# A residual transformer block on one core: the first slab of the up projection taken on tokens that carry no norm factor yet

## The chip, the cores and the metric

The kernel runs on 1 core of one Trainium2 chip. The metric is the device time of one execution in microseconds (us), the median of several runs. The engines are PE (TensorE, products), ACT (ScalarE), DVE (VectorE), POOL (GpSimd) and SP (the queue that issues the transfers).

## The reference

256 tokens of width 1024 pass a first block (two kinds of attention, a gated convolution feed-forward part, a gated embedding) and a second block (convolution, sparse attention, pooling, a mixture of 32 experts). The change lies at the start of the first block's feed-forward part:

```
x = x + rms_norm(mix, g_post_mix[i])

h = rms_norm(x, g_pre_ffn[i])
u = causal_depthwise_conv(h @ w_up[i], conv_w[i], conv_b[i])
gate, val = jnp.split(u, 2, axis=-1)
f = (jax.nn.gelu(gate, approximate=True) * val) @ w_down[i]
```

`rms_norm(x, g)` is `x * g` times one factor per token, 1/sqrt(mean(x*x) + eps). The factor depends on the token alone, so `(x * g) @ w_up` may be multiplied by it afterwards.

## The kernel before

Each engine has its own hand-written list of instructions, and they meet only through semaphores. Every engine runs its list in order, so an instruction that waits holds back all that is written behind it on its engine. There is no planner: the order in the code is the order on the chip.

**The tokens** lie with features on the partitions: `xT` has 8 tiles of 128 features x 256 tokens (in the trace the name is `xg`, which holds it). After the output projection `wo`, PE turns its result over, 16 products of 128x128 (`to_features`), and DVE adds it to `xT` tile by tile (`add_turned`, 8 instructions). Then the norm: ACT squares `xT` in 4 pieces, PE sums them with a matrix of ones (`token_sums`), ACT copies the sums, PE makes a column of them (`token_columns`), ACT takes the root, DVE its reciprocal, and PE spreads the factor over all partitions (`turned_over`, bank 3). DVE then makes `h` = x * gain * factor per tile (yT).

**Rounded pairs.** The large products run on operands rounded to fp32r, in two parts: a rounded one (hi, made by ACT) and the rest (lo, the original minus hi, made by DVE or POOL). One product of two numbers is three: hi*hi, hi*lo, lo*hi. So each tile of `h` has an `x_hi` (ACT) and an `x_lo` (DVE).

**The up projection** `w_up` comes in 11 slabs (j), each of 8 tiles (k) of 128 rows x 512 columns. Per tile ACT rounds the weights (`up_rounded`, 128x512), DVE or, for the tiles in `POOL_UP`, POOL makes the rest, and PE runs 12 products of 128x256. The rounded weights have 4 places (`weight_place`, two in `fr`, two in `fr_h`), so tile n is rounded only when PE has done with tile n-4. A slab's result fills two PSUM banks (`up_bank`): half 0 (gate) and half 1 (value). In slab j+1 its convolution follows (`conv_step` on three engines): ACT makes a base for each half (`conv_base`), DVE adds 2 taps to each half (`conv_tap`, 8 instructions per slab), ACT takes the gelu of half 0, POOL multiplies the halves (f), ACT rounds f (`f_hi`), POOL makes its rest (`f_lo`). The bank is free for slab j+2 after that.

**After slab 0** ACT also takes the silu of a vector (`crow`) that SP loads into `sq` when the norm's squares have been read. SP issues the loads of the slabs 3 to 6 behind that one. `mod_sum(1)` (a DVE copy) and `mod_total(1)` (PE, then DVE) finish a second vector product that only needs the slots of an earlier stage; before, they stand in the gap of the norm. `idle_products` are products whose result nobody reads.

Of the kernel before, what the change touches and what calls it, by code (L numbers as in the profile page):

```python
# [15 lines left out]
S = 256  # L16
# [45 lines left out]
POOL_UP = {("lo", 0, k) for k in (0, 1, 2, 3, 5, 7)} | {("lo", j, k) for j in range(1, 11) for k in (3, 7)}  # L62
# [100 lines left out]
def build(nc, A, out):  # L163
    with ExitStack() as ctx:
# [118 lines left out]
        OB = (6, 7)  # L283

# [24 lines left out]
        FB = (0, 1, 4, 5)  # L309
# [12 lines left out]
        def up_bank(j, part_):  # L322
            return FB[(2 * j + part_) % 4]

# [149 lines left out]
        def tensor(pe):  # L474
# [35 lines left out]
            def mod_total(s, *free):  # L510
                pe.wait_ge(dve_mod["sum", s], *free)
                for c in range(4):
                    t = pe.matmul(ps[:, 5, 4 * c:4 * c + 4], ar[:, modp + 128 * c:modp + 128 * c + 128], ident[:, 0:128:32], True, True)
                t.then_inc(pe_mod, "total", s)
# [255 lines left out]
            pe.wait_ge(act_wo["root", 1])  # L770
            idle_products(1, 5)
            token_sums("mix", 2, dve_joint["mix", "mt", 1, 0])
            idle_products(1, 5)
            token_columns("mix", 2)
            idle_products(2, 5)
            pe.wait_ge(dve_joint["mix", "rrecip"])
            turned_over(3, misc[:, 118:120]).then_inc(pe_joint, "mix", "over")
            mod_total(1, act_wo["root", 1])


            for j in range(11):
# [61 lines left out]
            embed(0, 0, dve_up["conv", 9, 1])  # L843
            pe.wait_ge(dve_up["conv", 10, 1])
# [4 lines left out]
            mod_half(10, 0, dve_up["conv", 9, 1])  # L849
# [377 lines left out]
        def scalar(act):  # L1227
# [212 lines left out]
            x_squares("mix")  # L1440
            joint_row("mix", 2, 116)
            for k in range(8):
                act.wait_ge(dve_up["h", k])
                act.copy(tile(fr, k, XH), tile(yT, k)).then_inc(act_up, "x_hi", k)


            def conv_base(j, p):
                act.wait_ge(pe_up[j, 7], pool_up["f_lo", j - 2] if j > 1 else dve_up["x_lo", 7])
                for i in range(2):
                    f = 2 * j + i + 22 * p  # L1450
                    act.activation(conv_place(j, p)[:, S * i:S * i + S], half(up_bank(j, p), i), ACT.Identity, scale=col("conv_w", 88 + f),
# [249 lines left out]
        def vector(dve):  # L1701
# [144 lines left out]
            def mod_total(s):  # L1846
                turned = ps[:, 5, 0:16].rearrange("p (c q) -> p q c", q=4)
# [103 lines left out]
            mod_total(1)  # L1951
# [15 lines left out]
            def conv_tap(j, p, d):  # L1967
                for i in range(2):
                    f = 2 * j + i + 22 * p
                    y, u = conv_place(j, p)[:, S * i:S * i + S], half(up_bank(j, p), i)  # L1970
# [14 lines left out]
            for j in range(11):  # L1985
                for k in range(8):
                    if ("lo", j, k) not in POOL_UP:
                        hi, lo = weight_place(8 * j + k)
                        dve.wait_ge(act_up["hi", j, k])
                        dve.tensor_tensor(lo, slot("wup", j)[:, 512 * k:512 * k + 512], hi.bitcast(F32), ALU.subtract).then_inc(dve_up, "lo", j, k)  # L1990
                    if j:
# [827 lines left out]
```

## Time and profile before

| what | value |
|---|---|
| median of 3 runs | 926.48 us (925.8 to 926.95) |
| span of the profiled execution, first to last instruction | 923.0 us |
| the runs' median over the span: 926.48 - 923.0 | 3.5 us |
| busy share PE / DVE / ACT / POOL | 85% / 41% / 35% / 14% |
| instructions | 12738 |

The profile is one execution. Its span is what the trace shows; the 3.5 us are what lies around the span in a run, and the page gives no time of its own for the profiled execution beside it. Busy shares are means over stages with different limits. A row of the timeline is a start, a duration, the engine, the code line, the operation with its result and inputs, and a count; in brackets stands the idle time of that engine before it and what ended it. A product in plain fp32 shows as two records.

### The profile page before, as it was taken

The numbers are of one execution on the slowest core, as the hardware profiler recorded it, in microseconds if no ns is written. First come the engines' busy times: TensorE is split into PE (matmuls) and PEld (weight loads), VectorE is DVE, ScalarE is ACT, GpSimd is POOL, SyncE is SP. The second block draws the span as 40 slices with busy tenths as digits, with TensorE's granted clock in tenths as the row PEclk, the third lists the DMA queues.
The fourth block names the chain that finished last, engine by engine and source line by source line (L and its number), as shares of the span: only waits on it lengthen the run. The fifth ranks groups of instructions, "written<-read, shape, count | busy, mean of one in ns | idle before, by whom it ended". The sixth has DMA issues, their size and how long they took to land.

```text
span 923.0 us, 12738 instructions
## 1 busy us (share of the span) xinstructions
PE 780.4 (85%) x5320; PEld 527.5 (57%) x5320; DVE 382.2 (41%) x837; ACT 327.2 (35%) x652; POOL 126.1 (14%) x129
## 2 busy tenths in 40 slices
PE   9999999999999999999999996567765576755756
PEld 7986588999998867798785432122220222211214
DVE  5747766667779764899613110010100101001002
ACT  5756756666665466824723010001000000000003
POOL 0011031555541034102110000000000000000000
PEclk9999999999999999999999999887797888979868
DMA  9956708754069782655679999999999999999996
GB/s 356 416 186 229 320 0 356 277 185 184 28 250 397 298 318 93 251 184 205 240 288 357 428 426 430 426 428 427 430 426 426 430 429 426 427 430 430 425 426 250
DMA packets 25263, 298.48 MB, mean 323 GB/s; under 512 B 2800, under 2 KB 3184, under 8 KB 6512
## 3 DMA queue, kind: packets, MB, share of 16 engines
q1 hardware_dynamic: 25200, 297.61, 78.5%
q8 instruction: 43, 0.70, 0.3%
q14 instruction: 20, 0.16, 0.1%
HBM read 296.55 MB, written 1.05 MB: 322 GB/s over the span
## 4 chain that ended last, share of the span: by engine, by line
PE 59%; DMA 33%; ACT 4%; DVE 3%; issue 1%; SPq 0%; DVEq 0%; ACTq 0%
PE ps L108 58%; DMA ring<-in_exps 33%; ACT fr L117 1%; PE ps L111 1%; ACT sq L114 1%; ACT ar L117 1%; ACT ar L114 0%; DVE ar L126 0%; DVE fr L126 0%; ACT L114 0%; DVE xg L134 0%; DVE yT L134 0%; DVE misc L149 0%; DVE yT L126 0%; DVE yT L130 0%
## 5 line engine op out<-in xcount | busy, mean ns | idle before, releaser
L108 PE MATMUL ps<-fr 128*128 128x256 f32 (+2 forms) x1308 | 206.6, 314 | 1.4 <-ACT fr L114 0.4
L108 PE MATMUL ps<-ring,sq 128*32 128x512 f32 x944 | 137.7, 719 | 78.3 <-DMA ring<-in_exps 77.9
L108 PEld LDWEIGHTS ps<-fr 128*128 128x128 f32 (+1 forms) x1308 | 182.9, 189 | 19.4 <-DVE fr L126 2.2
L108 PE MATMUL ps<-ring,ar 128*32 128x512 f32 (+4 forms) x792 | 93.5, 562 | 41.2 <-DMA ring<-in_exps 35.0
L108 PEld LDWEIGHTS ps<-ring,sq 128*32 128x32 f32 x944 | 28.7, 120 | 174.4 <-DMA ring<-in_exps 121.4
L126 DVE TENSOR_TENSOR fr<-ring,fr 128x512 fp32r<-128x512 f32 (+2 forms) x121 | 93.8, 804 | 42.9 <-ACT fr L117 42.6
L126 DVE TENSOR_TENSOR ar<-ar,ps 128x512 f32<-128x512 f32 x9 | 6.2, 687 | 254.4 <-PE ps L108 254.4
L117 ACT ACTIVATE fr<-ring 128x512 fp32r<-128x512 f32 (+1 forms) x139 | 80.1, 622 | 25.3 <-PE ps L108 23.1
L117 ACT ACTIVATE ar<-ps 128x512 f32<-128x512 f32 (+4 forms) x48 | 27.2, 571 | 171.2 <-PE ps L111 147.9
L108 PEld LDWEIGHTS ps<-ring,ar 128*32 128x32 f32 (+1 forms) x792 | 26.2, 117 | 93.5 <-DMA ring<-in_exps 53.1
L108 PE MATMUL ps<-ar 128*128 128x512 f32 (+10 forms) x328 | 66.4, 421 | 7.9 <-DVE ar L126 6.8
L126 DVE TENSOR_TENSOR ar<-ps,ar 128x512 f32<-128x512 f32 (+6 forms) x38 | 23.4, 633 | 108.8 <-PE ps L108 108.5
L114 ACT ACTIVATE sq<-ps,misc 128x128 f32<-128x128 f32 x31 | 11.9, 457 | 158.4 <-PE ps L108 158.4
L108 PE MATMUL ps<-fr,fr_h 128*128 128x256 f32 x528 | 66.9, 283 | 0.0
L108 PEld LDWEIGHTS ps<-fr,fr_h 128*128 128x128 f32 x528 | 64.9, 192 | 0.0
L108 PEld LDWEIGHTS ps<-ar 128*128 128x128 f32 (+4 forms) x328 | 37.1, 173 | 39.6 <-issue 19.2
L126 POOL TENSOR_TENSOR ar<-ar 128x128 f32<-128x128 f32 (+2 forms) x21 | 11.2, 535 | 310.8 <-DVE ar L126 309.7
L117 ACT ACTIVATE fr_h<-ring 128x512 fp32r<-128x512 f32 x66 | 40.2, 630 | 17.6 <-PE ps L108 17.6
L114 ACT ACTIVATE ar<-ps 128x768 f32<-128x768 f32 (+1 forms) x21 | 15.0, 717 | 81.1 <-PE ps L108 80.1
L108 PEld LDWEIGHTS ps<-ar,yT 128*128 128x128 f32 x256 | 32.6, 203 | 14.3 <-issue 14.1
L134 DVE SCALAR_TENSOR_TENSOR yT<-ps,cols,yT 128x255 f32<-128x255 f32 (+1 forms) x88 | 37.2, 474 | 0.0
L126 DVE TENSOR_TENSOR fr_h<-ring,fr_h 128x512 fp32r<-128x512 f32 x43 | 31.3, 730 | 13.5 <-ACT fr_h L117 13.5
(187 smaller groups left out, 908.9 us busy)
## 6 DMA issues: line engine op xcount, KB each, us to landing
ring<-in_exps SPq DMA_DIRECT2D x84, 2048.0 KB, 30.8
ring<-in_modw SPq DMA_DIRECT2D x12, 2048.0 KB, 13.1
ring<-in_wup SPq DMA_DIRECT2D x11, 2048.0 KB, 12.7
ring<-in_wdown SPq DMA_DIRECT2D x5, 2048.0 KB, 13.1
ring<-in_exps SPq DMA_DIRECT2D x9, 1024.0 KB, 10.4
ring<-in_win SPq DMA_DIRECT2D x4, 2048.0 KB, 11.3
ar<-in_exps SPq DMA_DIRECT2D x3, 2048.0 KB, 12.6
ring<-in_wo SPq DMA_DIRECT2D x2, 2048.0 KB, 8.7
```

The source lines that it names most:

```text
L108: return Issue(self.e and self.e.matmul(o, l, r, start=start, stop=stop, skip_group_check=True))
L111: return Issue(self.e and self.e.transpose(o, i, ident))
L114: return Issue(self.e and self.e.activation(o, i, f, **kw))
L117: return Issue(self.e and self.e.activation(o, i, ACT.Copy, scale=scale))
L126: return Issue(self.e and self.e.tensor_tensor(o, a, b, op))
L134: return Issue(self.e and self.e.scalar_tensor_tensor(out=o, in0=a, scalar=s, in1=b, op0=op0, op1=op1))
```

## The change

Slab 0 takes its products on x * gain without the token's factor ("raw": `raw_hi` on ACT, `raw_rest` on DVE), so PE can begin it as soon as x is there. In slab 0 the norm's factor is made: ACT squares x between the raw tiles, POOL adds the 4 pieces of squares to one (3 instructions), PE makes the columns from it between tiles 5 and 6 (`mix_columns`) and spreads the factor between tiles 6 and 7. DVE copies the factor row to SBUF (`rb`), multiplies the two halves of slab 0's result by it (`raw_out`, 2 instructions, into SBUF in place of PSUM), and makes `h` for the slabs 1 to 10, whose `x_hi` and `x_lo` are made within slab 1. So in slab 1, too, PE runs lo products of the tokens last in each tile. The convolution of slab 0 moves: its bases into slab 1, its taps, gelu, product and f into slab 2, beside those of slab 1, and they read SBUF (`ar`) and not PSUM. The silu moves behind slab 3. POOL now has the tiles 0 to 3 of slab 0 and 0 to 3 and 7 of slab 1. `mod_sum(1)` and `mod_total(1)` move up into the `wo` stage, the idle products go, and SP's wait before `crow` and the slabs 3 to 6 is now for the columns.

```diff
-POOL_UP = {("lo", 0, k) for k in (0, 1, 2, 3, 5, 7)} | {("lo", j, k) for j in range(1, 11) for k in (3, 7)}
+POOL_UP = {("lo", 0, k) for k in range(4)} | {("lo", 1, k) for k in range(3)} | {("lo", j, k) for j in range(1, 11) for k in (3, 7)}
...
-        FB = (0, 1, 4, 5)
+        RH, RL = 11264, 13312
+        FB = (4, 5, 0, 1)
...
+        def up_out(j, part_):
+            return bank(up_bank(j, part_)) if j else ar[:, RH + 512 * part_:RH + 512 * part_ + 512]
...
                         column_sums(5, [(tile(sq, k), act_wo["osq", k // 2]) for k in range(4)]).then_inc(pe_wo, "sums", 1)
+                        mod_total(1)
                         pe.wait_ge(act_wo["sums", 1])
...
-            pe.wait_ge(act_wo["root", 1])
-            idle_products(1, 5)
-            token_sums("mix", 2, dve_joint["mix", "mt", 1, 0])
-            idle_products(1, 5)
-            token_columns("mix", 2)
-            idle_products(2, 5)
-            pe.wait_ge(dve_joint["mix", "rrecip"])
-            turned_over(3, misc[:, 118:120]).then_inc(pe_joint, "mix", "over")
-            mod_total(1, act_wo["root", 1])
...
+            def mix_columns():
+                pe.wait_ge(pool_joint["mix", "squares", 3])
+                for j in range(2):
+                    for m in range(2):
+                        o = 256 * m + 128 * j
+                        t = pe.matmul(ps[:, 2, S + j:S + j + 1], sq[:, o:o + 128], ones[:, 0:1], j == 0 and m == 0, m == 1)
+                t.then_inc(pe_joint, "mix", "cols")
...
-                    if j == 0:
-                        pe.wait_ge(act_up["x_hi", k])
+                    xh, xl = (tile(fr, k, o) for o in ((XH, XL) if j else (RH, RL)))
+                    if j < 2:
+                        pe.wait_ge(act_up["x_hi" if j else "raw_hi", k])
                     for m in range(4):
...
-                            pe.wait_ge(dve_up["conv", j - 2, m // 2] if j > 1 else
-                                       (dve_mod["mod", 1] if m // 2 else dve_mod["sum", 1]) if j else dve_joint["mix", "x", 7])
+                            pe.wait_ge(*((dve_up["conv", j - 2, m // 2],) if j > 2 else (dve_up["raw", m // 2],) if j == 2 else
+                                         (dve_joint["mix", "x", 7],) if j else (dve_mod["mod", 1], act_wo["root", 1])))
...
-                        xh, xl = tile(fr, k, XH), tile(fr, k, XL)
...
-                        if j:
+                        if j > 1:
...
-                        t = pe.matmul(o, wl[:, c], xh, False, j > 0 and k == 7)
-                    if j == 0:
-                        pe.wait_ge(dve_up["x_lo", k])
+                        t = pe.matmul(o, wl[:, c], xh, False, j > 1 and k == 7)
+                    if j < 2:
+                        pe.wait_ge(dve_up["x_lo" if j else "raw_lo", k])
...
-                            t = pe.matmul(o, wh[:, c], tile(fr, k, XL), False, k == 7)
+                            t = pe.matmul(o, wh[:, c], xl, False, k == 7)
...
                     t.then_inc(pe_up, j, k)
+                    if (j, k) == (0, 5):
+                        mix_columns()
+                    if (j, k) == (0, 6):
+                        pe.wait_ge(dve_joint["mix", "rrecip"])
+                        turned_over(3, misc[:, 118:120]).then_inc(pe_joint, "mix", "over")
...
-            x_squares("mix")
-            joint_row("mix", 2, 116)
-            for k in range(8):
...
+            def raw_input(k):
+                act.wait_ge(dve_joint["mix", "x", k])
+                act.copy(tile(fr, k, RH), tile(xT, k), col("g_pre_ffn", k)).then_inc(act_up, "raw_hi", k)
...
+            for i in range(4):
+                raw_input(2 * i)
+                raw_input(2 * i + 1)
+                act.activation(sq[:, i * 512:(i + 1) * 512], xT[:, i * 512:(i + 1) * 512], ACT.Square).then_inc(act_joint, "mix", "xsq", i)
+                if i:
+                    up_rounded(0, 3 + i)
+            up_rounded(0, 7)
+            up_rounded(1, 0)
+            act.wait_ge(pe_joint["mix", "cols"])
+            row_root(misc[:, 116:118], ps[:, 2, S:S + 2], 1024).then_inc(act_joint, "mix", "rroot")
+            up_rounded(1, 1)
...
-                act.wait_ge(pe_up[j, 7], pool_up["f_lo", j - 2] if j > 1 else dve_up["x_lo", 7])
+                act.wait_ge(pool_up["f_lo", j - 2] if j > 1 else None, pe_up[j, 7] if j else dve_up["raw", p],
+                            dve_up["x_lo", 7 if j else 2 * p + 1])
...
-            for j in range(11):
+            normed_input(0)
+            up_rounded(1, 2)
+            normed_input(1)
+            normed_input(2)
+            up_rounded(1, 3)
+            conv_base(0, 0)
+            normed_input(3)
+            up_rounded(1, 4)
+            normed_input(4)
+            conv_base(0, 1)
+            up_rounded(1, 5)
+            normed_input(5)
+            normed_input(6)
+            up_rounded(1, 6)
+            normed_input(7)
+            up_rounded(1, 7)
+            for j in range(2, 11):
                 for k in range(8):
-                    if j or k > 3:
-                        up_rounded(j, k)
-                    if j:
-                        conv_step(j - 1, k)
-                if j == 0:
+                    up_rounded(j, k)
+                    if j == 2 and k in (2, 5):
+                        conv_step(0, 5 if k == 2 else 7)
+                    conv_step(j - 1, k)
+                if j == 3:
                     act.wait_ge(landed["crow"]["all"])
...
             mod_total(0)
+            mod_sum(1)
...
             group_factor(1)
+            mod_total(1)
...
-            for k in range(8):
-                add_turned("mix", k, (6, 7, 0, 1)[k // 2], col("g_post_mix", k))
-            joint_row("mix", 116)
-            mod_sum(1)
...
+            def raw_rest(k):
+                dve.wait_ge(act_up["raw_hi", k])
+                dve.scalar_tensor_tensor(tile(fr, k, RL), tile(xT, k), col("g_pre_ffn", k), tile(fr, k, RH).bitcast(F32),
+                                         ALU.mult, ALU.subtract).then_inc(dve_up, "raw_lo", k)
+
+            def raw_out(p):
+
+                dve.wait_ge(pe_up[0, 7], dve_joint["mix", "row"])
+                dve.tensor_tensor(by(up_out(0, p), S), by(bank(up_bank(0, p)), S), wide(rb[:, 1, :], 2), ALU.mult).then_inc(dve_up, "raw", p)
+
+            def normed(k):
+                dve.wait_ge(dve_joint["mix", "row"])
+                dve.scalar_tensor_tensor(tile(yT, k), tile(xT, k), col("g_pre_ffn", k), rb[:, 1, :], ALU.mult, ALU.mult).then_inc(dve_up, "h", k)
+
+            def normed_rest(k):
+                dve.wait_ge(act_up["x_hi", k])
+                dve.tensor_tensor(tile(fr, k, XL), tile(yT, k), tile(fr, k, XH).bitcast(F32), ALU.subtract).then_inc(dve_up, "x_lo", k)
...
+            def up_rest(j, k):
+                if ("lo", j, k) not in POOL_UP:
+                    hi, lo = weight_place(8 * j + k)
...
             for k in range(9):
                 if k < 8:
-                    dve.wait_ge(pe_joint["mix", "over"])
-                    dve.scalar_tensor_tensor(tile(yT, k), tile(xT, k), col("g_pre_ffn", k), half(3, 0), ALU.mult, ALU.mult).then_inc(dve_up, "h", k)
+                    add_turned("mix", k, (6, 7, 0, 1)[k // 2], col("g_post_mix", k))
                 if k:
-                    dve.wait_ge(act_up["x_hi", k - 1])
-                    dve.tensor_tensor(tile(fr, k - 1, XL), tile(yT, k - 1), tile(fr, k - 1, XH).bitcast(F32), ALU.subtract).then_inc(
-                        dve_up, "x_lo", k - 1)
-            mod_total(1)
+                    raw_rest(k - 1)
+                if k == 6:
+                    up_rest(0, 4)
+            for k in range(5, 8):
+                up_rest(0, k)
+            joint_row("mix", 116)
...
-            for j in range(11):
+            dve.wait_ge(pe_joint["mix", "over"])
+            dve.tensor_copy(rb[:, 1, :], half(3, 0)).then_inc(dve_joint, "mix", "row")
+            normed(0)
+            for k in range(1, 9):
+                if k < 8:
+                    normed(k)
+                normed_rest(k - 1)
+                if k in (2, 3):
+                    raw_out(k - 2)
+                if k in (4, 5, 6):
+                    up_rest(1, k)
+            for j in range(2, 11):
...
+                    up_rest(j, k)
+                    if j == 2 and k < 3:
+                        for d in ((1, 2), (1,), (2,))[k]:
+                            conv_tap(0, int(k > 0), d)
+                    conv_step(j - 1, k)
...
-            for j in range(11):
+            for k in range(4):
+                t = rest(pool_up, ("lo", 0, k), slot("wup", 0)[:, 512 * k:512 * k + 512], *weight_place(k), t, act_up["hi", 0, k])
+            for i in range(1, 4):
+                pool.wait_ge(t, act_joint["mix", "xsq", i])
+                t = pool.tensor_tensor(sq[:, 0:512], sq[:, 0:512], sq[:, 512 * i:512 * i + 512], ALU.add).then_inc(pool_joint, "mix", "squares", i)
+            for j in range(1, 11):
...
-                    if j:
+                    if j > 1:
+                        if j == 2 and k in (4, 6):
+                            t = conv_step(0, 6 if k == 4 else 7, t)
                         t = conv_step(j - 1, k, t)
...
-                    sp.wait_ge(pe_joint["mix", "sums"])
+                    sp.wait_ge(pe_joint["mix", "cols"])
```

On DVE, behind the turning over at the end of `wo`; `xg<-ps,cols,xg` is an add of `add_turned`, `fr<-xg,cols,fr` a `raw_rest`, `fr<-ring,fr` and `fr_h<-ring,fr_h` the rest of a weight tile of slab 0:

```order
-L134 SCALAR_TENSOR_TENSOR xg<-ps,cols,xg 128x256 x8
+L134 SCALAR_TENSOR_TENSOR xg<-ps,cols,xg 128x256 x2
...
+L134 SCALAR_TENSOR_TENSOR fr<-xg,cols,fr 128x256
+L126 TENSOR_TENSOR fr<-ring,fr 128x512
+L134 SCALAR_TENSOR_TENSOR xg<-ps,cols,xg 128x256
+L134 SCALAR_TENSOR_TENSOR fr<-xg,cols,fr 128x256 x2
+L126 TENSOR_TENSOR fr<-ring,fr 128x512
+L126 TENSOR_TENSOR fr_h<-ring,fr_h 128x512 x2
 L137 RECIPROCAL misc<-misc 128x2
```

The adds were one run of 8; now each is followed by a raw rest, and the rests of the weight tiles 4 to 7 stand among and behind them.

On POOL, from the rests of slab 0's first tiles on; `sq<-sq` are the adds of the squares, `yT<-yT` a product f of the convolution, `fr<-yT,fr` its rest:

```order
 L126 TENSOR_TENSOR fr_h<-ring,fr_h 128x512 x2
-L126 TENSOR_TENSOR fr<-ring,fr 128x512
-L126 TENSOR_TENSOR fr_h<-ring,fr_h 128x512 x2
+L126 TENSOR_TENSOR sq<-sq 128x512 x3
+L126 TENSOR_TENSOR fr<-ring,fr 128x512 x2
+L126 TENSOR_TENSOR fr_h<-ring,fr_h 128x512 x4
 L126 TENSOR_TENSOR yT<-yT 128x512
-L126 TENSOR_TENSOR fr_h<-ring,fr_h 128x512
 L126 TENSOR_TENSOR fr<-yT,fr 128x512
-L126 TENSOR_TENSOR fr_h<-ring,fr_h 128x512
 L126 TENSOR_TENSOR yT<-yT 128x512
 L126 TENSOR_TENSOR fr_h<-ring,fr_h 128x512
```

Two products f and the first f's rest now stand before tile 7 of slab 2 (the last `fr_h` row), with no weight tile between them.

On ACT, first a piece of slab 2, then what stands at the end of slab 3; `fr<-ring` and `fr_h<-ring` are weight tiles (the two `fr_h` rows around the first table load are the tiles 2 and 3 of slab 2), `yT<-yT` is a gelu, `fr<-yT` an `f_hi`, `sq<-sq` the silu:

```order
+L117 ACTIVATE fr_h<-ring 128x512
+L114 ACT_TABLE_LOAD
+L114 ACTIVATE yT<-yT 128x512
+L117 ACTIVATE fr_h<-ring 128x512
...
+L117 ACTIVATE fr<-yT 128x512
 L114 ACT_TABLE_LOAD
 L114 ACTIVATE sq<-sq 128x1024
...
 L117 ACTIVATE fr<-ring 128x512 x2
 L114 ACT_TABLE_LOAD
```

Before, the silu with its load stood behind slab 0, ahead of the first gelu and its load; now the load for slab 0's gelu comes first, between two weight tiles, then the silu's behind slab 3 and ahead of slab 4's weights, then a gelu's again: one load more.

## Rows read from the trace of the kernel before

**Rows 1.** The page's chain that ended last, by engine.

```profile
PE 59%; DMA 33%; ACT 4%; DVE 3%; issue 1%; SPq 0%; DVEq 0%; ACTq 0%
```

**Rows 2.** Busy time in stretches: start:end, length, PE, PEld, DVE, ACT, POOL, clock, DMA share, GB/s.

```profile
137.30:144.34 7.04, 6.19 (x44) 3.63 (x42) 3.97 (x11) 3.64 (x8) 0.77 (x1) 1.00 0.38 126
144.34:156.28 11.94, 11.83 (x97) 11.63 (x97) 8.60 (x19) 8.23 (x15) 2.92 (x2) 1.00 1.01 432
156.28:167.80 11.52, 11.52 (x99) 11.52 (x97) 7.37 (x14) 8.66 (x15) 5.70 (x4) 1.00 1.01 430
167.80:179.30 11.50, 11.50 (x98) 11.50 (x97) 8.02 (x15) 7.36 (x14) 5.80 (x5) 1.00 0.53 190
```

**Rows 3.** The chain in order of time: start, duration, what.

```profile
150.43 200.57 PE ps L108 x1374
...
553.36 30.16 DMA ring<-in_exps
```

**Rows 4.** Timeline of PE around the norm.

```profile
113.61 0.70 PE L108 MATMUL ps<-sd,con 128*128 128x256 f32 x2 [0.94 <-ACT sd L117]
...
137.37 0.39 PE L108 MATMUL ps<-con 128*128 128x128 f32 x2
...
142.51 0.71 PE L108 MATMUL ps<-con,misc 128*128 128x128 f32 x4
143.10 1.06 PE L108 MATMUL ps<-con,ar 128*128 128x4 f32 x8
144.34 3.11 PE L108 MATMUL ps<-fr 128*128 128x256 f32 x24 [0.18 <-ACT fr L117]
```

**Rows 5.** Timeline of DVE and POOL, a later stage with the raw rest's form.

```profile
335.87 4.10 POOL L126 TENSOR_TENSOR fr<-ring,fr 128x512 fp32r<-128x512 f32 x3
...
337.35 0.47 DVE L134 SCALAR_TENSOR_TENSOR xg<-ps,cols,xg 128x256 f32<-128x256 f32 x1
337.74 1.09 DVE L134 SCALAR_TENSOR_TENSOR fr<-xg,cols,fr 128x256 fp32r<-128x256 f32 x1
...
340.57 0.47 DVE L134 SCALAR_TENSOR_TENSOR fr<-xg,cols,fr 128x256 fp32r<-128x256 f32 x1
```

**Rows 6.** Timeline of ACT, a later stage with the raw tile's form.

```profile
336.07 0.91 ACT L117 ACTIVATE fr<-xg,cols 128x256 fp32r<-128x256 f32 x2
```

**Rows 7.** Timeline of DVE, slabs 0 and 1, and the adds before them.

```profile
136.30 3.23 DVE L134 SCALAR_TENSOR_TENSOR xg<-ps,cols,xg 128x256 f32<-128x256 f32 x8 [0.87 <-PE ps L108]
...
144.22 0.43 DVE L126 TENSOR_TENSOR fr<-yT,fr 128x256 fp32r<-128x256 f32 x1
...
150.72 1.43 DVE L126 TENSOR_TENSOR fr_h<-ring,fr_h 128x512 fp32r<-128x512 f32 x1 [0.35 <-ACT fr_h L117]
154.14 1.29 DVE L126 TENSOR_TENSOR fr<-ring,fr 128x512 fp32r<-128x512 f32 x2 [1.99 <-ACT fr L117]
158.67 1.64 DVE L134 SCALAR_TENSOR_TENSOR yT<-ps,cols,yT 128x255 f32<-128x255 f32 x4
```

**Rows 8.** Timeline of POOL, slabs 0 and 1.

```profile
150.31 1.29 POOL L126 TENSOR_TENSOR fr<-ring,fr 128x512 fp32r<-128x512 f32 x1 [12.25 <-ACT fr L117]
...
163.25 1.60 POOL L126 TENSOR_TENSOR yT<-yT 128x512 f32<-128x512 f32 x1 [3.26 <-DVE yT L134]
164.92 1.29 POOL L126 TENSOR_TENSOR fr_h<-ring,fr_h 128x512 fp32r<-128x512 f32 x1
```

**Rows 9.** Timeline of ACT, slabs 0 and 1.

```profile
151.23 1.28 ACT L114 ACT_TABLE_LOAD   x1
152.53 1.06 ACT L114 ACTIVATE sq<-sq 128x1024 f32<-128x1024 f32 x1
...
165.41 1.14 ACT L117 ACTIVATE fr<-ring 128x512 fp32r<-128x512 f32 x2
168.00 1.02 ACT L114 ACTIVATE yT<-ps,cols 128x256 f32<-128x256 f32 x2 [1.45 <-PE ps L108]
```

**Rows 10.** Timeline of SP.

```profile
141.28 1.90 SPq L160 DMA_DIRECT2D ring<-in_wup  x4
```

More of the change, by code:

```diff
@@ L283, in build @@
         OB = (6, 7)
+        TOTAL_BANK = (5, 4, 5)
         part_place = [fr[:, vm:vm + 1024], fr_r[:, 2048:3072], fr_r[:, 3072:4096], fr[:, wT:wT + 1024], fr[:, vS:vS + 1024],
@@ L512, in mod_total @@
                 for c in range(4):
-                    t = pe.matmul(ps[:, 5, 4 * c:4 * c + 4], ar[:, modp + 128 * c:modp + 128 * c + 128], ident[:, 0:128:32], True, True)
+                    t = pe.matmul(ps[:, TOTAL_BANK[s], 4 * c:4 * c + 4], ar[:, modp + 128 * c:modp + 128 * c + 128], ident[:, 0:128:32], True, True)
                 t.then_inc(pe_mod, "total", s)
@@ L841, in gate @@
                 pe.matmul(o, xh, wl, False, k == 7).then_inc(pe_gate, j, n, k)
-            embed(0, 0, dve_up["conv", 9, 1])
-            pe.wait_ge(dve_up["conv", 10, 1])
+            embed(0, 0, dve_up["conv", 10, 1])
             to_features("ffn", (0, 1, 2, 3))
@@ L848, in tensor @@
             embed(1, 1, act_gate["e", 1, 0])
-            mod_half(10, 0, dve_up["conv", 9, 1])
+            mod_half(10, 0)
             pe.wait_ge(act_gate["e", 1, 1], dve_joint["ffn", "mt", 1, 1])
@@ L1439, in scalar, with normed_input @@
             up_rounded(0, 3)
-            x_squares("mix")
-            joint_row("mix", 2, 116)
-            for k in range(8):
+            def raw_input(k):
+                act.wait_ge(dve_joint["mix", "x", k])
+                act.copy(tile(fr, k, RH), tile(xT, k), col("g_pre_ffn", k)).then_inc(act_up, "raw_hi", k)
+            def normed_input(k):
                 act.wait_ge(dve_up["h", k])
                 act.copy(tile(fr, k, XH), tile(yT, k)).then_inc(act_up, "x_hi", k)
+            for i in range(4):
[9 more added lines that the diff above has]
+            up_rounded(1, 1)
             def conv_base(j, p):
-                act.wait_ge(pe_up[j, 7], pool_up["f_lo", j - 2] if j > 1 else dve_up["x_lo", 7])
+                act.wait_ge(pool_up["f_lo", j - 2] if j > 1 else None, pe_up[j, 7] if j else dve_up["raw", p],
+                            dve_up["x_lo", 7 if j else 2 * p + 1])
                 for i in range(2):
                     f = 2 * j + i + 22 * p
-                    act.activation(conv_place(j, p)[:, S * i:S * i + S], half(up_bank(j, p), i), ACT.Identity, scale=col("conv_w", 88 + f),
+                    act.activation(conv_place(j, p)[:, S * i:S * i + S], up_out(j, p)[:, S * i:S * i + S], ACT.Identity, scale=col("conv_w", 88 + f),
                                    bias=col("conv_b", f)).then_inc(act_up, "base", j, p, i)
@@ L1846, in mod_total @@
             def mod_total(s):
-                turned = ps[:, 5, 0:16].rearrange("p (c q) -> p q c", q=4)
+                turned = ps[:, TOTAL_BANK[s], 0:16].rearrange("p (c q) -> p q c", q=4)
                 o = (mod[:, 32:48] if s else mod[:, 16:32]).rearrange("p (q c) -> p q c", c=4)
@@ L1943, in vector @@
+            def up_rest(j, k):
+                if ("lo", j, k) not in POOL_UP:
+                    hi, lo = weight_place(8 * j + k)
+                    dve.wait_ge(act_up["hi", j, k])
+                    dve.tensor_tensor(lo, slot("wup", j)[:, 512 * k:512 * k + 512], hi.bitcast(F32), ALU.subtract).then_inc(dve_up, "lo", j, k)
             for k in range(9):
                 if k < 8:
-                    dve.wait_ge(pe_joint["mix", "over"])
-                    dve.scalar_tensor_tensor(tile(yT, k), tile(xT, k), col("g_pre_ffn", k), half(3, 0), ALU.mult, ALU.mult).then_inc(dve_up, "h", k)
+                    add_turned("mix", k, (6, 7, 0, 1)[k // 2], col("g_post_mix", k))
@@ L1969, in conv_tap @@
                     f = 2 * j + i + 22 * p
-                    y, u = conv_place(j, p)[:, S * i:S * i + S], half(up_bank(j, p), i)
+                    y, u = conv_place(j, p)[:, S * i:S * i + S], up_out(j, p)[:, S * i:S * i + S]
                     dve.wait_ge(act_up["base", j, p, 1] if d == 1 else dve_up["tap", j, p, i])
@@ L1983, in conv_step @@
                     conv_tap(j, 1, 2)
-            for j in range(11):
-                for k in range(8):
[L1987 to L1990, printed above, removed]
-                    if j:
-                        conv_step(j - 1, k)
+            dve.wait_ge(pe_joint["mix", "over"])
[10 more added lines that the diff above has]
+            for j in range(2, 11):
+                for k in range(8):
+                    up_rest(j, k)
[3 more added lines that the diff above has]
+                    conv_step(j - 1, k)
                     if j > 6 and k == 1:
@@ L2343, in gpsimd @@
                                  act_up["hi", j, k])
-                    if j:
+                    if j > 1:
+                        if j == 2 and k in (4, 6):
+                            t = conv_step(0, 6 if k == 4 else 7, t)
                         t = conv_step(j - 1, k, t)
```

## Prediction

> **What bounds the kernel now.** I read the chain that ended last first. By engine it is PE for 59% and DMA for 33% [rows 1]; in order of time it is PE without a break from 150.43 us for 200.57 us, and from 553.36 us on it is the loads of the expert weights [rows 3]. So the stretch that the change touches is bound by PE. The loads at the end are issued as PE gives places of the ring free, so a shift of PE at 150 us should move their start, and the end, by as much; I take one to one.
>
> The stretches say how full PE is [rows 2]. In 137.30 to 144.34, the norm, PE shows 6.19 us busy, but with idle products, sums and columns. Slab 0 runs from 144.34 to 156.28, slab 1 to 167.80, slab 2 to 179.30. In slabs 1 and 2 PE is busy the whole time, 96 products in 11.5 us or 0.12 us each, at the full clock (granted 1.00). The other engines have 11.5 us per slab, too, and DVE's 8.02 and POOL's 5.80 hide only as long as each result comes in time. How much time that is, is the question here.
>
> **What is removed.** PE ends the turning over at 137.37 and begins slab 0 at 144.34 [rows 4]. The first raw tile is ready about then: the adds begin at 136.30 and take 0.40 each (3.23 for 8) [rows 7], a raw tile on ACT takes some 0.42 (0.91 for 2 in a row) [rows 6]. So slab 0 can begin at 137.4: **-7.0 us**.
>
> **What is added on PE.** The columns: 4 products, 8 records, near the row of 8 small ones, 1.06 [rows 4]: 1.0. The spreading, 0.71 for 4 records [rows 4]: 0.6 until the next product. `mod_total(1)`, 1.06 [rows 4], moves into a wait of 0.94 ahead of 113.61 [rows 4], with a DVE copy ahead of the group norm. Between 0.1 (1.06 - 0.94) and 0.8 (a copy of 0.7 all on the path, plus that); I take 0.2, since PE has 84 products of old tiles to run meanwhile.
>
> **What it does to the others.** No row shows the new order, so I lay it out: every engine's list in its written order, each instruction starting when its engine is free and its last input is there. Durations from rows, back to back: DVE 0.40 for 128x256 with a scalar, 0.61 for 128x512 (1.29 for 2, where 0.69 and 0.60 follow each other, an overlap of some 0.08), and by that overlap 0.35 for the plain subtraction of 0.43 [rows 7]; ACT 0.52 for a weight tile (1.14 for 2), 0.45 for a base (1.02 for 2) [rows 9]; POOL 1.30 [rows 8]. Laid out so, the old order gives slab ends of 156.3, 167.8, 179.4 and 190.9; the rows have 156.28, 167.80, 179.30, so the layout carries such waits.
>
> One more thing goes into it. DVE and POOL hold each other up. A DVE instruction with two tensors in SBUF, the raw rest's form, takes 0.47 alone and 1.09 while POOL works; one with a PSUM input takes 0.47 beside the same POOL work [rows 5]. The weight rest at 150.72 takes 1.43 and ends after POOL's at 150.31 to 151.60 [rows 7, 8]. The change makes many such instructions: 8 raw rests, `h` from the copied row in SBUF and not from PSUM, 8 taps of slab 0 from SBUF, and 3 adds on POOL that did not exist. Of `h` and the taps no row shows that they are held. The Trainium skill ("SBUF — State Buffer", "Who interferes with whom") has any DVE instruction with two SBUF inputs contend with a GpSimd one that reads SBUF, and none with one SBUF input. By the row's two forms alone the layout ends 0.4 us earlier than by that rule; I take all of them as held.
>
> - *Slab 0.* Before tile 4's weight rest DVE has 7 adds and 6 raw rests (5.2 us from 136.30), waits 0.3 and 0.55 for ACT's raw tiles, which stand behind squares and weight tiles, and is held by two of POOL's adds (0.4 and 1.1). The rest is done at 144.36, PE wants it at 143.1: 1.26. Tile 5's is behind another add and two raw rests, 0.60 late. Slab 0 ends at 137.37 + 11.52 + 1.26 + 0.60 + 1.6 + 0.1 = 152.5, **3.8 us ahead** of 156.3.
> - *Slab 1.* The factor leaves PE at 151.0, the row copy and the first `h` and `x_hi` take 1.4, 0.1 of it on PE. Then DVE has 8 `h`, 8 `x_lo`, 2 raw outputs, 3 weight rests, 3.2 + 2.8 + 1.2 + 1.8 = 9.0 us of 11.5, with 2 us of being held and a turn to ACT and back for each tile. PE waits 0.44 for the third `x_lo`, 0.28, 0.72 and 1.46 for the weight rests of tiles 5, 6 and 7: tile 7 is rounded behind the last `x_hi`, at 164.0, and POOL adds 1.3. Sum 3.0; the slab ends at 167.0, **0.8 ahead**.
> - *Slab 2.* ACT loads the gelu's table, 1.28 [rows 9], and runs slab 0's gelu between the weight tiles 2 and 3: tile 3 is 1.19 late. DVE has 16 taps (8 take 3.3 by 1.64 for 4 [rows 7]), so slab 1's product f comes late on POOL, and tile 7 behind it: 1.14; tile 6 0.26. In the old order POOL's tile 7 ends at 166.21 [rows 8] for a PE that wants it at 166.4, so there was 0.2 to give. Sum 2.6, the end at 181.15, **1.8 behind**.
> - *Slab 4.* In the old order the first weight tiles of a slab are rounded at 165.41, 2.4 before the slab begins at 167.80 [rows 2, 9], and need 0.63 and a DVE rest of 0.69. Table load and silu, 1.28 + 1.0 [rows 9], now stand ahead of them: 2.3 + 1.3 - 2.4 = **1.2 late**. Before, they stood at 151.23, where ACT then waited for PE. For a table switch the Trainium skill ("ScalarE: Activation LUTs", "Table sets: the hidden batching unit") gives some 2.7 us, an estimate of 2.4 us more on the sum; the trace has 1.28, and the sum goes by that.
>
> SP's loads of slabs 3 to 6, at 141.28 [rows 10], go out behind the columns, some 8 us later; slab 3's weights are wanted at about 178, so 30 us hide it; without that cover it is the 8.
>
> Sum: slab 4 ends 1.8 + 1.2 = 3.0 us later than before, and nothing changes behind it. With the 0.2 of `wo`, **+3.2 us**. On the profiled span, 923.0 + 3.2 = 926.2; the runs lie 3.5 above it, so **929.7 us**, 0.35% slower. With the durations moved by 2 to 6% the layout's +3.0 stays within 2.4 and 3.9.
>
> **Rivals.**
> 1. *DVE and POOL don't hold each other in the new places.* Without any of it the layout ends 1.2 ahead, with `wo` 1.0: 925.5 us. For it: no row shows `h` or the taps beside POOL. Against it: the raw rest's own form is held [rows 5], and weight rests are [rows 7]. If POOL's adds of the squares alone escape, +1.7, 928.2.
> 2. *PE stays fed, faster.* The waits of the slabs 1, 2 and 4 (3.0 + 2.6 + 1.2 = 6.8) are each a chain of small handovers between ACT, DVE and POOL. If the weight rests come early enough, only slab 0's costs remain: -3.8 + 0.2 = -3.6, 922.9 us. It decides once those waits fall under 1.7 together, for then it is over 0.2% faster. For it: DVE and ACT are not full over a slab [rows 2]. Against it: the order is fixed, and the slack of POOL's tile 7 was 0.2 us.
> 3. *The delay does not reach the end.* From 553.36 the loads bound [rows 3]; had they been issued ahead of need, a late PE would cost nothing: 926.5. Against it: they are issued when PE frees their places.
>
> **How the numbers follow.** A difference of 0.2% (1.9 us) is about what a measurement of this kernel tells from none. The forecast, with its own range of 928.6 to 930.7, has 0.68, rival 1 0.14, rival 2 0.14, rival 3 0.04. A hundredth of rival 1 lies beyond the bound, at partial holding. So slower 0.69, same 0.17, faster 0.14. The range leaves rival 2 out and reaches down to rival 1, 925.4, and up to 931.3, the layout's worst and 0.8 in `wo`.
>
> **What the profile will show.** Right: PE's first `fr` products at 137.4 to 137.6; slab 0 (its end by the first wait for `raw_out`) at 152 to 153; PE waiting 3 us in slab 1 and over 2 in slab 2, for POOL in the last tile of each; 1 us ahead of slab 4, for ACT and DVE behind the silu; raw rests of over 1 us beside POOL's adds. From slab 5 on 11.5 us per slab. Wrong: slab 1 ending before 165, raw rests and `h` at 0.47 beside POOL, or no wait ahead of slab 4; then the layout's handovers are too slow. A longer `wo` stage would show as a turning over that ends later than 137.6.

## The result and the profile after

The changed kernel takes 930.22 us (median of 5 runs, 928.75 to 931.38) against 926.48 (925.8 to 927.2, 5 runs): the ratio is 1.004 with a 95% interval of 1.0028 to 1.0052, or 3.7 us more. Slower was the likeliest forecast, at 929.7. One of the nine executions of the kernel without POOL's adds, below, took 1486.27 us; its ratio leaves that one out, and the median of the other eight is 928.20 for 928.30.

The page's chain that ended last, by engine, answers to [rows 1]; PE has lost four points of it, most of them to ACT and DVE (5% each, for 4% and 3%).

```profile
PE 55%; DMA 33%; ACT 5%; DVE 5%; POOL 1%; issue 1%; POOLq 0%; DVEq 0%; ACTq 0%
```

The chain in order of time shows what took them: where before it was PE alone from 150.43 us [rows 3], it now goes from engine to engine, mostly one short instruction each, and PE has it alone only from 195.14 on. Its DMA tail begins at 557.84 instead of 553.36 [rows 3].

```profile
164.33 0.63 ACT fr_h L117
165.09 1.28 POOL fr_h L126
166.41 1.71 PE ps L108 x12
...
195.14 160.27 PE ps L108 x1038
...
557.84 30.40 DMA ring<-in_exps
```

The timeline of PE, answering to [rows 4]: a bracket is the idle time ahead of the row and what ended it.

```profile
107.24 1.05 PE L108 MATMUL ps<-con,ar 128*128 128x4 f32 x8
...
138.26 3.15 PE L108 MATMUL ps<-fr 128*128 128x256 f32 x24
...
145.63 1.69 PE L108 MATMUL ps<-fr 128*128 128x256 f32 x12 [1.35 <-DVE fr L126]
147.69 1.70 PE L108 MATMUL ps<-fr 128*128 128x256 f32 x12 [0.38 <-DVE fr L126]
149.23 0.95 PE L108 MATMUL ps<-con,sq 128*128 128x1 f32 x8
150.04 1.67 PE L108 MATMUL ps<-fr,fr_h 128*128 128x256 f32 x12
151.56 0.60 PE L108 MATMUL ps<-con,misc 128*128 128x128 f32 x4
...
163.63 1.69 PE L108 MATMUL ps<-fr,fr_h 128*128 128x256 f32 x12 [0.41 <-DVE fr_h L126]
166.41 1.69 PE L108 MATMUL ps<-fr,fr_h 128*128 128x256 f32 x12 [1.10 <-POOL fr_h L126]
...
173.63 1.70 PE L108 MATMUL ps<-fr,fr_h 128*128 128x256 f32 x12 [1.21 <-POOL fr_h L126]
...
180.71 1.70 PE L108 MATMUL ps<-fr,fr_h 128*128 128x256 f32 x12 [0.83 <-POOL fr_h L126]
...
195.14 3.13 PE L108 MATMUL ps<-fr 128*128 128x256 f32 x24 [1.22 <-DVE fr L126]
...
218.26 3.04 PE L108 MATMUL ps<-fr 128*128 128x256 f32 x24
```

Slab 0 begins right behind the turning over, at 138.26, and holds the columns (149.23) and the spreading (151.56). The waits that follow are for DVE in slab 0, DVE and POOL in slab 1, POOL twice in slab 2, and DVE ahead of slab 4. In the same view of the kernel before, the row that answers to 107.24 (the first vector product's total, ahead of the `wo` stage) and slab 6's first row stand here:

```profile
106.46 1.05 PE L108 MATMUL ps<-con,ar 128*128 128x4 f32 x8
...
213.85 3.04 PE L108 MATMUL ps<-fr 128*128 128x256 f32 x24
```

So 0.78 of the delay is there at 107.24, ahead of every instruction that the change moves. The kernels below that have the whole change stand at 106.70 to 106.97 in that row; where those 0.2 to 0.8 come from stays open. They are left out by measuring from the end of the turning over, 137.37 before [rows 4] and 138.26 after, to slab 6: 76.48 before, 80.00 after, 3.52 us more. In the two profiles slab 6 begins 4.41 later (218.26 for 213.85) and the DMA tail 4.48 later.

The busy time by slab, with the columns of [rows 2]:

```profile
138.26:153.74 15.48, 13.62 (x110) 13.03 (x109) 13.61 (x23) 9.09 (x20) 7.69 (x6) 1.00 0.19 50
153.74:167.94 14.20, 12.58 (x96) 11.77 (x97) 12.40 (x23) 8.76 (x19) 4.07 (x3) 1.00 1.01 427
167.94:182.24 14.30, 12.27 (x98) 11.67 (x97) 10.72 (x21) 9.82 (x17) 8.81 (x6) 1.00 1.00 426
182.24:193.76 11.52, 11.52 (x98) 11.48 (x96) 6.28 (x13) 8.59 (x15) 5.60 (x5) 1.00 0.53 205
193.76:206.75 12.99, 11.77 (x98) 11.61 (x97) 9.24 (x16) 9.79 (x18) 5.98 (x4) 1.00 0.45 161
```

The slabs last 15.48, 14.20, 14.30, 11.52 and 12.99 us where PE needs 11.52 for the products of one, at the same granted clock of 1.00. In slab 2 no engine is full: DVE has 10.72 and ACT 9.82 of 14.30. In the slabs 0 and 1 DVE's 13.61 and 12.40, which include the time that POOL held it up, are more than 11.52; whether PE waits there for single late results or for an engine out of time, these rows do not decide, and the runs with other orders below do.

Last, DVE beside POOL in this stage, in its timeline:

```profile
143.41 1.28 POOL L126 TENSOR_TENSOR sq<-sq 128x512 f32<-128x512 f32 x1 [0.55 <-ACT sq L114]
143.46 1.51 DVE L134 SCALAR_TENSOR_TENSOR fr<-xg,cols,fr 128x256 fp32r<-128x256 f32 x1
...
144.90 0.68 DVE L126 TENSOR_TENSOR fr<-ring,fr 128x512 fp32r<-128x512 f32 x1
...
147.18 1.60 POOL L126 TENSOR_TENSOR sq<-sq 128x512 f32<-128x512 f32 x1 [2.49 <-ACT sq L114]
147.59 3.42 DVE L126 TENSOR_TENSOR fr_h<-ring,fr_h 128x512 fp32r<-128x512 f32 x2
148.86 1.60 POOL L126 TENSOR_TENSOR fr<-ring,fr 128x512 fp32r<-128x512 f32 x1
...
154.61 2.88 POOL L126 TENSOR_TENSOR fr_h<-ring,fr_h 128x512 fp32r<-128x512 f32 x2 [2.18 <-ACT fr L117]
154.80 0.69 DVE L126 TENSOR_TENSOR ar<-ps,rb 128x512 f32<-128x512 f32 x1
...
155.40 0.92 DVE L134 SCALAR_TENSOR_TENSOR yT<-xg,cols,rb 128x256 f32<-128x256 f32 x1
...
156.24 1.52 DVE L126 TENSOR_TENSOR fr<-yT,fr 128x256 fp32r<-128x256 f32 x1
```

A raw rest, 0.47 alone, lasts 1.51 while POOL adds squares, and the weight rest for which PE waits until 145.63 stands right behind it. An `h` lasts 0.92 and an `x_lo` 1.52 beside POOL's weight rests at 154.61, while the raw output at 154.80, beside the same POOL work but with an input in PSUM, takes 0.69, what a weight rest of its size takes alone. By the Trainium skill ("SBUF — State Buffer", "Who interferes with whom") a DVE instruction with two inputs in SBUF contends with a GpSimd one that reads SBUF, and one with at most one such input does not, outside of DVE's 2-port modes, an exception that the prediction did not say; these rows agree.

### The profile page after: what moved, and what is told of

Same layout as the page of the kernel before. It is cut to its first block, busy times and chain, and to the rows that moved or that the text cites. A ratio compares the mean times of both kernels' runs of the same rounds, so it can differ in the third digit from the quotient of the medians.

```text
span 928.9 us, 12731 instructions
## 1 busy us (share of the span) xinstructions
PE 776.3 (84%) x5300; PEld 524.2 (56%) x5300; DVE 390.4 (42%) x847; ACT 331.6 (36%) x660; POOL 131.4 (14%) x133
## 4 chain that ended last, share of the span: by engine, by line
PE 55%; DMA 33%; ACT 5%; DVE 5%; POOL 1%; issue 1%; POOLq 0%; DVEq 0%; ACTq 0%
PE ps L108 54%; DMA ring<-in_exps 33%; ACT fr L117 1%; DVE yT L134 1%; DVE fr L126 1%; ACT L114 1%; ACT sq L114 1%; PE ps L111 1%; DVE ar L126 1%; ACT yT L114 1%; POOL yT L126 1%; ACT ar L117 0%; ACT ar L114 0%; DVE fr L134 0%; POOL fr_h L126 0%
## 5 line engine op out<-in xcount | busy, mean ns | idle before, releaser
L126 DVE TENSOR_TENSOR fr<-ring,fr 128x512 fp32r<-128x512 f32 (+1 forms) x120 | 92.0, 795 | 43.4 <-ACT fr L117 43.2
L108 PE MATMUL ps<-ar 128*128 128x512 f32 (+10 forms) x328 | 62.3, 407 | 8.0 <-DVE ar L126 6.9
L126 POOL TENSOR_TENSOR fr_h<-ring,fr_h 128x512 fp32r<-128x512 f32 x23 | 30.0, 1304 | 41.3 <-ACT fr_h L117 38.2
```

What stands on the lines that cost most here:

```text
L108: return Issue(self.e and self.e.matmul(o, l, r, start=start, stop=stop, skip_group_check=True))
L126: return Issue(self.e and self.e.tensor_tensor(o, a, b, op))
```

## The experiments

The theory: the raw first slab itself saves about what the prediction gave it; the delay comes from single results that arrive late in a fixed order, some of them because POOL and DVE hold each other up. The rivals: the engines have no room for the added work in slabs 1 and 2 whatever the order; or one of the terms (POOL's adds, the silu, the moved total) costs nothing, its wait being taken by the next.

**The move into `wo` alone.** On the kernel before:

```diff
                         column_sums(5, [...]).then_inc(pe_wo, "sums", 1)
+                        mod_total(1)
...
-            mod_total(1, act_wo["root", 1])
```

> The kernel before with one part of the change alone: the copy and the four products of the second modulation total stand in the stage of wo. My theory (the wait ahead of PE's group norm hides them): PE's transposes of the mix begin within 0.1 us of the 133.36 of before, slab 0 begins within 0.3 us of 144.34, since the total stood there beside the first norm's h and x_hi, and the time is 926.5 within 1. The rival (they lie on the path, the upper bound of the prediction's term): the transposes begin 0.8 later and the time is 927.3 or more.

Measured 925.59 (ratio 0.9996, 0.9986 to 1.0005). PE's timeline:

```profile
137.41 0.39 PE L108 MATMUL ps<-con 128*128 128x128 f32 x2
...
144.37 3.11 PE L108 MATMUL ps<-fr 128*128 128x256 f32 x24 [1.11 <-ACT fr L117]
```

The turning over ends at 137.41 for 137.37, and slab 0 begins at 144.37 for 144.34 [rows 4]. The move costs nothing, and taken alone it gains nothing either: PE waits 1.11 for ACT where `mod_total(1)` stood. The expected 0.1 at most held.

**Without POOL's adds.** On the changed kernel; the factor is then made of the first quarter of the squares alone, and three quarters of the sum are left out:

```diff
-                pe.wait_ge(pool_joint["mix", "squares", 3])
+                pe.wait_ge(act_joint["mix", "xsq", 3])
...
-            for i in range(1, 4):
-                pool.wait_ge(t, act_joint["mix", "xsq", i])
-                t = pool.tensor_tensor(sq[:, 0:512], sq[:, 0:512], sq[:, 512 * i:512 * i + 512], ALU.add)...
```

> The changed kernel without POOL's three adds of the squares; the factor is made of the first quarter of the squares alone, so this part of the sum is left out, and everything else is done as before. My theory (the adds cost nothing themselves, but hold DVE's raw rests and weight rests up): no raw rest over 0.6 us, PE's waits for the weight rests of tiles 4 and 5 (1.35 and 0.38 us) fall to 0.3 together, slab 0 lasts 14.0 us in place of 15.48, and as much reaches the end: 928.7 in place of 930.2. Rival 1 (the waits come from the written order alone, DVE and POOL don't matter to each other here): slab 0 lasts 15.2 to 15.5, the time stays at 930. Rival 2 (slab 1's own chain absorbs it: PE waits there for the same work): slab 0 is 1.5 shorter, slab 1 as much longer, 930.

Measured 928.30 (ratio 1.0022, 1.0011 to 1.0032), 1.9 less than the changed kernel. The timeline, DVE at the place of the held rests and PE:

```profile
137.82 0.98 DVE L134 SCALAR_TENSOR_TENSOR fr<-xg,cols,fr 128x256 fp32r<-128x256 f32 x1 [0.19 <-ACT fr L117]
...
142.81 0.48 DVE L134 SCALAR_TENSOR_TENSOR fr<-xg,cols,fr 128x256 fp32r<-128x256 f32 x1
143.20 0.69 DVE L126 TENSOR_TENSOR fr<-ring,fr 128x512 fp32r<-128x512 f32 x1
...
143.94 1.69 PE L108 MATMUL ps<-fr 128*128 128x256 f32 x12
...
146.00 1.70 PE L108 MATMUL ps<-fr 128*128 128x256 f32 x12 [0.36 <-DVE fr L126]
```

And PE alone, in slab 2:

```profile
172.17 1.70 PE L108 MATMUL ps<-fr,fr_h 128*128 128x256 f32 x12 [1.55 <-POOL fr_h L126]
```

The raw rests beside which POOL added now have 0.48, the weight rest begins at 143.20 instead of 144.90, and PE's 1.35 at tile 4 is gone; tile 5's wait is still there with 0.36. Slab 0 lasts 14.16 (137.89 to 152.05), 1.32 less. So in this order it is the holding that made tile 4 late, and not the order alone. One raw rest of 0.98 is left, beside POOL's weight rest of tile 3, which the expectation had forgotten. Slab 2's first wait for POOL grew from 1.21 to 1.55, so a little is taken back.

**The silu earlier.** On the changed kernel:

```diff
+                    if (j, k) == (3, 7):
+                        act.wait_ge(landed["crow"]["all"])
+                        act.activation(sq[:, 0:1024], sq[:, 0:1024], ACT.Silu)...
                     conv_step(j - 1, k)
-                if j == 3:
-                    ...
```

> The changed kernel with ScalarE's table load and silu moved from behind slab 3's last weight tile to the place ahead of slab 2's rounded product, where ScalarE waits some 2 us for POOL. My theory (ahead of slab 4 they keep its first weight tiles waiting 1.2 us, and PE has nothing else): PE's wait of 1.22 us at 193.9 goes, slab 4 lasts 11.6 us in place of 12.99, and the end comes 1.2 us earlier, 929.0. The rival (the loads at the end don't wait for PE, or the wait moves to the product's consumer): slab 4 is shorter but a wait of the same size stands in slab 3 or 5, or the start of the DMA tail at 557.84 doesn't move; 930.2.

Measured 929.14 (ratio 1.0031, 1.0019 to 1.0043). By the medians that is 1.1 less than the changed kernel; the intervals of the two overlap, so the place is what decides:

```profile
193.72 3.14 PE L108 MATMUL ps<-fr 128*128 128x256 f32 x24 [0.23 <-DVE fr L126]
```

The wait ahead of slab 4 is 0.23 where it was 1.22, and the slabs 5 and 6 begin 11.62 and 11.52 us after the ones before them, so the wait has not moved there. Table and silu were on the path.

**Tile 7 earlier.** On the changed kernel, the weight tiles 6 and 7 of slab 1 are rounded ahead of the last two normed inputs:

```diff
             normed_input(5)
-            normed_input(6)
             up_rounded(1, 6)
-            normed_input(7)
             up_rounded(1, 7)
+            normed_input(6)
+            normed_input(7)
```

> The changed kernel with one move: ScalarE rounds slab 1's weight tiles 6 and 7 ahead of the last two normed inputs and not between and behind them. My theory (PE's 1.10 us wait for GpSimd's rest of tile 7 begins on ScalarE, where the tile is rounded last): that wait falls under 0.3, slab 1 lasts 13.1 us in place of 14.20, nothing takes it back, and the time is 929.1 in place of 930.2. The rival (the rest is late for GpSimd's own queue and speed, or the last x_lo becomes what PE waits for): a wait of about 1 us stays in slab 1's last tiles, 930.

Measured 928.18 (ratio 1.0021, 1.0012 to 1.0030), 2.0 less than the changed kernel. PE:

```profile
153.46 3.11 PE L108 MATMUL ps<-fr 128*128 128x256 f32 x24
...
164.35 2.17 PE L108 MATMUL ps<-fr,fr_h 128*128 128x256 f32 x16 [0.45 <-DVE fr L126]
166.36 3.22 PE L108 MATMUL ps<-fr 128*128 128x256 f32 x24
```

Slab 1 lasts 12.90 (153.46 to 166.36) and not 14.20; of 0.41 and 1.10 us of waits one of 0.45 is left. The 1.10 that the trace put down to POOL began one engine further back, with ScalarE's order. The expectation had that wait under 0.3: the 0.45 is now for DVE, for the last two `x_lo`, which stand at 163.89 behind an `h` that lasts 1.51 (162.45) beside POOL's rest of tile 7 (161.97). So a part of the rival came with it, and the time is still lower than the 929.1 expected.

**All slabs laid out anew.** The layout of the prediction was used to search orders of the three engines' lists for slabs 0 to 5. On PE the columns stand after tile 4, the spreading after tile 5. The heads of the lists (`lo` is a weight rest, `sqadd` an add of squares, the numbers are slab and tile):

```diff
+ACT_LIST = (
+    "rawhi.0 rawhi.1 rawhi.2 sq.0 sq.1 rawhi.4 sq.2 rawhi.6 rawhi.3 hi.0.4 sq.3 rawhi.7 hi.0.5 hi.0.7 hi.0.6 "
...
+DVE_LIST = (
+    "x.0 x.1 x.2 rawlo.0 x.3 x.5 rawlo.1 x.4 x.7 x.6 rawlo.2 sqadd.2 rawlo.3 lo.0.4 rawlo.4 rawlo.7 sqadd.3 "
...
+POOL_LIST = (
+    "sqadd.1 lo.2.4 lo.2.5 lo.2.6 f.0 flo.0 f.1 lo.3.3 lo.3.7 flo.1 f.2 lo.4.3 f.3 lo.4.7 flo.2 flo.3 lo.5.3 "
```

> The changed kernel with the same instructions for the slabs 0 to 5, but ScalarE, VectorE and GpSimd in another written order, two of the three adds of squares on VectorE, slab 1's weight rests on VectorE and four of slab 2's spread over both, and the columns after tile 4. My theory (the raw slab itself is worth 7.0 less 1.6 us; all that was lost behind it are handovers that the order makes): laid out with the same durations PE waits 0.2 us in slab 0 and nowhere in the slabs 1 to 5, 8.5 us less than the changed kernel; the layout was 0.8 us too kind to the changed kernel by slab 5, so between 921.0 and 922.5 on the clock. The rival (the engines are too full in the slabs 1 and 2, the work of the factor's second copy of the tokens and of the taps has no room): waits of over 3 us remain in slabs 1 and 2 whatever the order, 925 or more.

Measured 920.47 (ratio 0.994, 0.9926 to 0.9953): 5.7 faster than before and 9.7 faster than the changed kernel, and a little faster than the 921.0 to 922.5 expected. The first three slabs as stretches:

```profile
137.86:150.96 13.10, 13.10 (x110) 13.01 (x110) 12.79 (x29) 9.93 (x21) 1.94 (x2) 1.00 0.28 100
150.96:162.48 11.52, 11.52 (x99) 11.52 (x98) 11.41 (x26) 8.44 (x19) 0.00 (x0) 1.00 1.01 431
162.48:174.00 11.52, 11.52 (x99) 11.52 (x98) 10.91 (x20) 9.00 (x16) 5.75 (x5) 1.00 1.01 430
```

PE is busy for the whole of each; the next three slabs last 11.86, 11.58 and 11.67. In slab 1 DVE is at 11.41 of 11.52 and still in time; POOL does nothing there (0.00) and holds nothing up. So the room was there; the rival that the engines are too full falls.

**The order alone.** The same search with the changed kernel's placement kept (all adds, and the rests of slab 1's tiles 0 to 3 and 7, on POOL); PE's columns and spreading are one tile earlier here too, which the expectation does not say. The lines are the difference from the re-laid kernel; the lists of ACT and DVE were searched anew with POOL's.

```diff
 POOL_LIST = (
-    "sqadd.1 lo.2.4 lo.2.5 lo.2.6 f.0 flo.0 f.1 ...
+    "sqadd.1 sqadd.2 sqadd.3 lo.1.0 lo.1.1 lo.1.2 lo.1.3 lo.1.7 lo.2.3 lo.2.7 f.0 flo.0 ...
```

> As the re-laid kernel, but every instruction stays on the engine that the changed kernel gives it: all three adds of the squares and the weight rests of slab 1's tiles 0 to 2 on GpSimd, so that only the written orders of ScalarE, VectorE and GpSimd differ from the changed kernel. My theory (order is most of it, the placement the rest): the layout gives 1.1 us of waits in slab 1 and 0.6 in slab 5, 1.8 in all beyond the re-laid kernel, so 922 to 923.5. The rival (the gain of the re-laid kernel is the work taken off GpSimd, which holds VectorE up): 926 or more, with waits for POOL in slabs 1 and 2 as in the changed kernel.

Measured 921.86 (ratio 0.9948, 0.9934 to 0.9961), where 922 to 923.5 was expected. PE's only waits of over 0.2 us in the six slabs:

```profile
151.71 3.10 PE L129 MATMUL ps<-fr 128*128 128x256 f32 x24 [0.75 <-ACT fr L138]
...
201.41 3.13 PE L129 MATMUL ps<-fr,fr_h 128*128 128x256 f32 x24 [0.28 <-DVE fr_h L147]
```

One of 0.75 ahead of slab 1, for the first normed tile, and one of 0.28 in slab 5. In slab 0 POOL's adds hold DVE up here, too (two weight rests from 142.86 on take 2.39), and PE begins tile 4 at 143.60 without a wait: what the holding costs hangs on the order. Of the 9.7 us between the changed and the re-laid kernel, order, with the place of columns and spreading, makes 8.4 (930.22 - 921.86), placement 1.4; against each one's kernel before, in the table below, it is 8.2 and 1.2.

## Why the prediction was right

**One to one to the end.** PE's stretch from the end of the turning over to slab 6, and the medians against the kernel before that ran beside it (us). The differences from the changed kernel's 930.22 that are given above are in this column 1.6 without POOL's adds, 0.75 for the silu and 1.9 for tile 7:

| kernel | stretch | against before | time against before |
|---|---|---|---|
| before | 76.48 | | |
| changed | 80.00 | +3.52 | +3.74 |
| `wo` alone | 76.50 | +0.02 | -0.56 |
| without POOL's adds | 78.70 | +2.22 | +2.15 |
| silu early | 79.01 | +2.53 | +2.99 |
| tile 7 early | 78.64 | +2.16 | +1.82 |
| order alone | 72.74 | -3.74 | -4.50 |
| re-laid | 71.25 | -5.23 | -5.68 |

All times follow the stretch within 0.8 us, over a spread of 9. The third rival (loads issued ahead of need) falls. The loads of the slabs 3 to 6, which SP now issues at 150.58 and not 141.28 [rows 10], kept nobody waiting: slab 3 lasts 11.52.

**`wo`:** forecast +0.2, measured 0.04 alone (137.41 for 137.37). In the changed kernel the turning over ends at 138.26. By its letter that is the prediction's sign of a longer `wo` stage (later than 137.6), but 0.78 of the 0.89 is there at 107.24; from that row on it is 31.02 for 30.91, 0.11 more.

**Slab 0:** forecast 3.8 ahead, and from the end of the turning over it is 3.4 (15.48 against 156.28 - 137.37 = 18.91 [rows 2, 4]). The two big waits were close, 1.26 and 0.60 forecast, 1.35 and 0.38 measured. Columns and spreading took 0.81 (149.23 to 150.04) and 0.36, 1.17 and not 1.6. The mis-sized term is the last 0.1: what is left of the slab is 15.48 - 11.52 - 1.73 (1.35 + 0.38) - 1.17 = 1.06. It lies in six places of 0.08 to 0.38 us between the rows, the longest ahead of slab 1; what each of them waits for is not shown.

**Slab 1:** 3.0 of waits forecast, 14.20 - 11.52 = 2.68 measured; the wait for tile 7 was forecast as 1.46, "rounded behind the last `x_hi`", and is 1.10 for that reason, as the moved tiles show.

**Slab 2:** 2.6 forecast, 2.78 measured, with tile 3 at 1.21 (forecast 1.19) and tile 7 at 0.83 (1.14), each ended by POOL. ACT's rows say why tile 3 is late:

```profile
169.71 1.28 ACT L114 ACT_TABLE_LOAD   x1
...
171.55 0.62 ACT L117 ACTIVATE fr_h<-ring 128x512 fp32r<-128x512 f32 x1
...
191.49 1.28 ACT L114 ACT_TABLE_LOAD   x1
192.78 1.06 ACT L114 ACTIVATE sq<-sq 128x1024 f32<-128x1024 f32 x1
```

The gelu's table load and the gelu (171.01) stand ahead of the tile's rounding at 171.55, and POOL's 1.27 (from 172.31) comes behind it. Tile 7's rest begins on POOL at 179.37, right behind the product f at 177.67, as forecast. That these two chains are the cause was read here; only the other orders, which have neither wait, bear on it, and no run moved one of them alone.

**Slab 4:** 1.2 forecast, 1.22 measured, behind the table load and silu at 191.49 and 192.78, as the early silu shows; with small waits behind it the slab is 1.47 too long (12.99 - 11.52). The load takes 1.28 here as in [rows 9]. The figure of the Trainium skill ("ScalarE: Activation LUTs", "Table sets: the hidden batching unit"), some 2.7 us for a switch, is not what this trace shows: the load stands at 191.49, right behind a rounding, and the silu begins at 192.78, 1.29 later.

**The sum:** 3.0 forecast for the slabs, 3.5 measured: slab 0 is 0.4 over its forecast (15.48 against 15.08), slab 2 0.2, slab 4 0.3, slab 1 0.3 under. With `wo` it was 3.2 against 3.7 on the clock. The sum is 0.5 off where these four misses add up to 1.2; that slab 1's took back most of slab 0's is luck. The 3.5 us that the forecast put on the span are not all time around it: the kernel's runs beside the experiments last 2.0 to 2.2 us longer than their spans, so the profiled execution before was some 1.4 quicker than the median. It did no harm, since the forecast is the median plus 3.2. And two bounds do not come out of their terms: 926.48 with 2.4 and 0.1 gives 929.0 and not 928.6, with 3.9 and 0.8 it gives 931.2 and not 931.3; the result does not hang on them.

**Rival 1**, no holding in the new places: wrong in all of them that POOL met. `h` and `x_lo` are held in the rows above. Slab 0's taps met no POOL work in the changed kernel, where the prediction took them as held, too, but in the re-laid one they did:

```profile
164.89 2.79 POOL L147 TENSOR_TENSOR fr<-ring,fr 128x512 fp32r<-128x512 f32 x2 [23.61 <-ACT fr L138]
...
165.69 0.87 DVE L155 SCALAR_TENSOR_TENSOR yT<-ps,cols,yT 128x255 f32<-128x255 f32 x2 [0.54 <-ACT yT L135]
...
166.48 2.91 DVE L155 SCALAR_TENSOR_TENSOR yT<-ar,cols,yT 128x254 f32<-128x254 f32 x2
```

Two taps with all inputs in SBUF take 2.91 beside POOL's weight rests; two with a PSUM input took 0.87 just before, beside the first of these rests. The price named for the adds alone, a time of 928.2 without them, was met by 928.3. A kernel without any holding was not run, so the rival's full price, 925.5, is not tested.

**Rival 2**, PE stays fed: not in this order, as forecast. But its mechanism is real. The prediction put it at 922.9, with slab 0's costs left; the re-laid kernel is at 920.5, mostly since its slab 0 lasts only 13.10 for the forecast's 15.08.

## What to carry to other kernels

A stage in which no engine but the bound one is full (DVE at 10.72 and ACT at 9.82 of slab 2's 14.30) can still lose a fifth of its time (14.30 for 11.52) when each result passes through three in-order engines: lay the lists out with the durations of the rows, and look at the first late tile of each slab, not at the sums. A wait that a trace puts down to POOL may begin on an engine before it, as slab 1's 1.10 did on ACT; follow it back to the last instruction that could have run sooner, and move that one. A change that removes a stall should come with new lists for what was hidden in it: the same change is worth +3.7 us, -4.5 with other orders alone, or -5.7 with other placement too.

## What the runs showed of the hardware

In these rows the holding hits DVE harder than POOL: POOL's add at 147.18 and weight rest at 148.86 take 1.60 each instead of 1.28, while DVE's two weight rests beside them take 3.42, where two alone take 1.29 [rows 7]. With POOL empty for one slab, as in the re-laid kernel, DVE did eight weight rests there besides the normed tiles and ended in time (11.41 of 11.52).
